# A split-precision encoder layer on one core: H in pairs of slots, three products of zeros at the start, and work moved forward on four engines

## The reference, cut to what matters

```python
h = x + W_o(sig(g_s5) * S5branch(xn) + sig(g_conv) * ConvBranch(xn))     # xn = RMSNorm(x)
h = h + CrossAttn(RMSNorm(h), RMSNorm(mem))                              # 256 rows of mem each
h = h + SwiGLU(RMSNorm(h))                                               # d_ff 2816

# S5 branch, per direction (forward, and backward with reverse=True); 32 groups of 16 channels, 64 states
A_bar = exp(A * dt);  B_bar = ((A_bar - 1) / A) * B
bu = einsum("gnp,blgp->blgn", B_bar, u)
h = scan(h[t] = A_bar * h[t-1] + bu[t])
y = einsum("gpn,blgn->blgp", C, h).real          # summed over the directions
y = gelu(y + d * u);  s5_out = (y @ w_glu_a) * sigmoid(y @ w_glu_b)
```

## Time and profile before

| | |
|---|---|
| median of 3 runs | 2540.95 us |
| the profiled execution | 2542.96 us |
| its span, mean granted TensorE clock | 2541.3 us, 0.988 |
| PE busy | 2451.0 us (96%), 12542 instructions |
| DVE, ACT, POOL busy | 1641.1, 765.8, 275.4 us (65, 30, 11%) |
| PE in the chain that ended last | 88%, DVE 3%, DMA 2% |

### The profile page before, as it was taken

How to read it: one execution, slowest core, us unless ns; L and a number is a source line. 1 busy time by engine, 2 the same in 40 slices (tenths; PEclk the granted TensorE clock), 3 DMA queues, 4 the chain that set the end, 5 groups by cost and what they waited for, 6 DMA issues and landing times.

```text
span 2541.3 us, 34409 instructions
## 1 busy us (share of the span) xinstructions
PE 2451.0 (96%) x12542; PEld 2201.0 (87%) x12542; DVE 1641.1 (65%) x2978; ACT 765.8 (30%) x1226; POOL 275.4 (11%) x283
## 2 busy tenths in 40 slices
PE   8999988799999999999999999999999999999997
PEld 6788866678888788888868999999999999999996
DVE  6735542358874397253264588888878687777777
ACT  5301110232222332130143244343343343332333
POOL 0078781000000021000000000010100000000000
PEclk9999998999999999999999999999999999999999
DMA  7332227542223743213231212132332621222212
GB/s 240 120 116 82 84 71 140 147 142 73 73 82 125 206 182 124 83 58 133 81 107 49 87 50 76 59 113 85 110 104 94 250 68 58 88 82 79 77 69 73
DMA packets 103801, 262.99 MB, mean 103 GB/s; under 512 B 15104, under 2 KB 46336, under 8 KB 103680
## 3 DMA queue, kind: packets, MB, share of 16 engines
q1 hardware_dynamic: 96736, 238.82, 29.1%
q0 software_dynamic: 6944, 22.55, 2.6%
HBM read 198.45 MB, written 64.98 MB: 104 GB/s over the span
## 4 chain that ended last, share of the span: by engine, by line
PE 88%; DVE 3%; DMA 2%; issue 1%; ACT 1%; SPq 0%; DVEq 0%; ACTq 0%
PE bank L735 27%; PE bank L737 27%; PE bank L736 27%; PE bank L1013 2%; PE bank L959 2%; PE bank L990 1%; DMA BBL<-scratch_BB 1%; PE bank L956 1%; PE bank L1002 0%; DVE EL L2133 0%; ACT EH L1176 0%; DVE HR L2446 0%; PE bank L901 0%; DMA ML<-scratch_M 0%; SPq L413 0%
## 5 line engine op out<-in xcount | busy, mean ns | idle before, releaser
L735 PE MATMUL bank<-XN,WLO 128*128 128x512 f32 x1152 | 449.3, 390 | 3.7 <-DVE WLO L1639 1.7
L737 PE MATMUL bank<-XN,WHI 128*128 128x512 f32 x1152 | 448.2, 389 | 0.0
L736 PE MATMUL bank<-XN,WHI 128*128 128x512 f32 x1152 | 448.2, 389 | 0.0
L735 PE MATMUL bank<-XH,EL 128*128 128x384 f32 x1232 | 412.4, 335 | 1.6 <-DVE U2T L2159 0.9
L737 PE MATMUL bank<-XH,EH 128*128 128x384 f32 x1232 | 411.5, 334 | 0.0
L736 PE MATMUL bank<-XL,EH 128*128 128x384 f32 x1232 | 411.5, 334 | 0.0
L735 PEld LDWEIGHTS bank<-XN,WLO 128*128 128x128 f32 x1152 | 216.2, 188 | 50.2 <-issue 3.1
L736 PEld LDWEIGHTS bank<-XN,WHI 128*128 128x128 f32 x1152 | 216.2, 188 | 45.1 <-issue 0.5
L737 PEld LDWEIGHTS bank<-XN,WHI 128*128 128x128 f32 x1152 | 216.2, 188 | 45.0
L735 PE MATMUL bank<-AF,EL 128*128 128x384 f32 x704 | 238.3, 338 | 9.7 <-DVE AF L1644 6.4
L736 PE MATMUL bank<-AF,EH 128*128 128x384 f32 x704 | 236.5, 336 | 0.0
(11 more groups left out here) (267 smaller groups left out, 3888.4 us busy)
## 6 DMA issues: line engine op xcount, KB each, us to landing
RAW<-W_all SPq DMA_DIRECT2D x132, 512.0 KB, 3.5
WR<-W_all SPq DMA_DIRECT2D x92, 512.0 KB, 4.5
scratch_G<-GS SPq DMA_DIRECT2D x16, 768.0 KB, 3.7
XS<-xT SPq DMA_DIRECT2D x8, 768.0 KB, 6.0
scratch_CO<-COS SPq DMA_DIRECT2D x8, 768.0 KB, 4.3
COL<-scratch_CO SPq DMA_DIRECT2D x8, 768.0 KB, 4.3
G2L<-scratch_G SPq DMA_DIRECT2D x8, 768.0 KB, 5.8
G1L<-scratch_G SPq DMA_DIRECT2D x8, 768.0 KB, 7.2
```

The source lines that it names most:

```text
L735: pe_mm(out, w[1], x[0], start=first, stop=False, skip_group_check=onto)
L736: pe_mm(out, w[0], x[1], start=False, stop=False, skip_group_check=onto)
L737: return pe_mm(out, w[0], x[0], start=False, stop=last, skip_group_check=onto)
```

## The change

- PE issues three products of zeros (128x512, f32) ahead of the first key product; DVE zeroes their operand first.
- DVE: the seven parts of the parameters stand between steps of kv (n is the slot), not behind it. ACT's two Sin stand in kv too.
- POOL: the first direction's loads of B and C are issued before the powers, the second's after its buffers are free.
- H holds pairs of slots, `[pair, column, 2]`: two neighbouring slots lie side by side. The copies into H are four per side instead of two (odd and even slots apart), the scan's operands have a stride of 8 bytes, the products of s5b read both slots of a pair, and ML's two products of 128 and 64 columns are one of 192. s5b's results go to banks 4 to 7, not 0 to 3.
- SP: the loads of s5a's first two iterations are issued in co, those of the others two iterations ahead. y comes back from DRAM in halves of a tile, YL lies elsewhere, and the parts of y's first tile lie in XN, so that it is split before s5b is through. The last iteration of glu is unrolled on ACT and DVE.
- FFN: in the last step of each group (`close=True`), the gated product of block 0 is made and split inside the step.

```diff
-    H = at("H", 0, [SLOTS, GD])
+    H = at("H", 0, [PAIRS, GD, 2])
...
+    def states_of(g, slot, n, odd):
+
+        pairs = slice((slot + 1 + odd) // 2, (slot + 1 + odd) // 2 + n // 2)
+        return H[:, pairs, bass.ds(g, 2), 1 - odd].rearrange("p s g -> p g s")
...
+    def y_part(low, k):
+
+        return YHL[:, low, k] if k else XN[:, low, KT - 1]
...
+        def load_v(it, par):
+            g = bass.ds(2 * it, 2)
+            sp.dma_start(VN[:, par], V_d[:, g, :, :].rearrange("p g d c -> p (g d) c")).then_inc(S(f"s5a_in{par}"), 16)
+
+        def load_w(it, par):
+            g = bass.ds(2 * it, 2)
+            sp.dma_start(WK[:, par].rearrange("p (g d) c -> p g d c", d=2),
+                         W_d[:, g, :].rearrange("p g (d c) -> p g d c", d=2)[:, :, :, 0:P]
+                         ).then_inc(S(f"s5a_in{par}"), 16)
+            sp.dma_start(BBL[:, par].rearrange("p (d g) c -> p d g c", d=2),
+                         BB_d[:, :, g, :].rearrange("d p g c -> p d g c")).then_inc(S(f"s5a_in{par}"), 16)
...
+            if j == 2:
+                for par in range(2):
+                    sp.wait_ge(S(f"tables_stored{par}"), 2 * 4 * 32)
+                sp.wait_ge(S("bb_stored"), 32)
+                for par in range(2):
+                    load_v(par, par)
+                    load_w(par, par)
...
-                if not (last and par):
-                    sp.wait_ge(S("states_bwd"), it)
-                    s5a_loads(it + 1, 1 - par)
+                if not last:
+                    sp.wait_ge(S("v_turned"), it + 1)
+                    load_v(it + 2, par)
+                    sp.wait_ge(S("lags"), it + 1)
+                    load_w(it + 2, par)
...
-        def load_y(k):
-
-            sp.wait_ge(S(f"y_stored{k}"), 32)
-            for g in range(P // GP):
+        def load_y(q):
+
+            k, half = q // 2, q % 2
+            sp.wait_ge(S(f"y_stored{k}"), 16 * (half + 1))
+            for g in range(4 * half, 4 * half + 4):
                 sp.dma_start(YL[GP * g:GP * (g + 1), k], y_rows[8 * k + g]).then_inc(S(f"y_in{k}"), 16)
...
         for q in range(quads):
+            if q:
+                load_y(q - 1)
             sp.wait_ge(S("y_made"), 2 * (q + 1))
             g = slice(QUAD * q, QUAD * (q + 1))
             sp.dma_start(Y_d[:, g, :], U[:, g, :]).then_inc(S(f"y_stored{q // 2}"), 16)
             if q + 2 < quads:
                 s5b_loads(q + 2)
-            if q % 2 == 0 and q:
-                load_y(q // 2 - 1)
...
+        for dst, src in ((BX, "BX"), (BY, "BY"), (CX, "CX"), (CY, "CY")):
+            pool.dma_start(dst[:], io[src][0]).then_inc(S("bc_in"), 16)
...
                 pool.wait_ge(S("bb_stored"), 16)
-            for dst, src in ((BX, "BX"), (BY, "BY"), (CX, "CX"), (CY, "CY")):
-                pool.dma_start(dst[:], io[src][d]).then_inc(S("bc_in"), 16)
-            pool.wait_ge(S("bc_in"), 64 * (d + 1))
+                pool.wait_ge(S("bc_in"), 96)
+                for dst, src in ((CX, "CX"), (CY, "CY")):
+                    pool.dma_start(dst[:], io[src][1]).then_inc(S("bc_in"), 16)
+            else:
+                pool.wait_ge(S("bc_in"), 64)
...
+            if d == 0:
+                for dst, src in ((BX, "BX"), (BY, "BY")):
+                    pool.dma_start(dst[:], io[src][1]).then_inc(S("bc_in"), 16)
...
+                    if d:
+                        pool.wait_ge(S("bc_in"), 128)
...
+        pe.wait_ge(S("vector_step"), 1)
+        for _ in range(3):
+            nc.tensor.matmul(PS[5][:], SQ[:, 0, 0:P], SQ[:, 0, 0:BLK], start=True, stop=True)
         key(0)
         key(1)
...
-                        pe.wait_ge(S("y_made"), 2 * (q - 1) + n + 1)
-                    out = PS[2 * par + n][:, g % 2 * NC:(g % 2 + 1) * NC]
-                    u = one(U, QUAD * q + g)
-                    for c0, n, slot in ((0, NCP, 0), (NCP, NCS, SLOT_S)):
-                        o = out[:, c0:c0 + n]
-                        nc.tensor.matmul(o, ML[par][:, g, :], u[:, c0:c0 + n], start=True, stop=False)
-                        for d in (1, 0):
-                            h = H[:, slot:slot + n, bass.ds(d * GROUPS + QUAD * q + g, 1)].rearrange("p s o -> p (s o)")
-                            last = nc.tensor.matmul(o[:, ::-1] if d else o,
-                                                    WO[par][:, g, d, :], h, start=False, stop=d == 0)
+                        pe.wait_ge(S("y_made"), 2 * q + n - 3)
+                    out = PS[4 + 2 * par + n][:, g % 2 * NC:(g % 2 + 1) * NC]
+                    nc.tensor.matmul(out, ML[par][:, g, :], one(U, QUAD * q + g), start=True, stop=False)
+                    for d in (1, 0):
+                        for c0, n, slot in ((0, NCP, 0), (NCP, NCS, SLOT_S)):
+                            o = out[:, c0:c0 + n]
+                            h = H[:, slot // 2:(slot + n) // 2, bass.ds(d * GROUPS + QUAD * q + g, 1), :]
+                            last = nc.tensor.matmul((o[:, ::-1] if d else o).rearrange("p (s t) -> p s t", t=2),
+                                                    WO[par][:, g, d, :], h.rearrange("p s o t -> p s (o t)"),
+                                                    start=False, stop=d == 0 and c0 > 0)
...
+        yin = lambda k, b: (y_part(0, k)[:, blk(b)], y_part(1, k)[:, blk(b)])
+        pe.wait_ge(S("y_made"), GROUPS // 2 - 2)
         first_half_pair("glu", lambda k: (S("y_lo"), k + 1), yin)
...
+            if n == KT + 4:
+                act.wait_ge(S("angles"), 2)
+                nc.scalar.activation(PA[:, 9, :], PA[:, 9, :], ACT.Sin).then_inc(S("sines"), 1)
+                nc.scalar.activation(PA[:, 10, :], PA[:, 10, :], ACT.Sin).then_inc(S("sines"), 1)
...
-            dst = H[:, :, bass.ds(d * GROUPS + 2 * it, 2)].rearrange("p s g -> p g s")
             src = src[:, 0:2 * NC].rearrange("p (g c) -> p g c", g=2)
-            for lo, n, c in ((1, NCP, 0), (SLOT_S + 1, NCS, NCP)):
-                copy(dst[:, :, lo:lo + n], src[:, :, c:c + n]).then_inc(signal, 1)
+            for slot, n, c in ((0, NCP, 0), (SLOT_S, NCS, NCP)):
+                for odd in range(2):
+                    dst = states_of(d * GROUPS + 2 * it, slot, n, odd)
+                    copy(dst, src[:, :, c + odd:c + n:2]).then_inc(signal, 1)
...
+        def y_split(k):
+
+            act.wait_ge(S(f"y_in{k}"), 128)
+            copy(y_part(0, k).rearrange("p (c t) -> p c t", t=C), YL[:, k].rearrange("p t c -> p c t")
+                 ).then_inc(S("y_hi"), 1)
+
         for it in range(GROUPS // 2):
             act.wait_ge(S("s5_out"), it + 1)
-            nc.scalar.activation(U[:, 2 * it:2 * it + 2, :], PS[it % 4][:, 0:2 * NC].rearrange(
+            nc.scalar.activation(U[:, 2 * it:2 * it + 2, :], PS[4 + it % 4][:, 0:2 * NC].rearrange(
...
+            if it == GROUPS // 4:
+                y_split(0)
...
+                if isinstance(i, int) and par:
+                    act.wait_ge(res, RES0["glu"] + 6 * KT)
...
+        with loop(nc.scalar, 3) as i:
+            glu(i)
+        glu(3)
...
+                if close and j == 6:
+                    act_hi(s, odd, 0)
...
+        then(V.memset(SQ[:, 0, 0:BLK], 0.0))
...
+            if n == 6:
+                parameters(0)
+                parameters(1)
+            if n == KT + 3:
+                parameters(2)
             if n == KT + 4:
                 values_out(0)
+            if n == KT + 5:
+                parameters(3)
+                parameters(4)
+            if n == 2 * KT - 1:
+                parameters(5)
+                parameters(6)
...
-        for part in range(5):
-            parameters(part)
...
-            if j == 0:
-                parameters(5)
-                parameters(6)
...
-            then(V.memset(H[:, slot, :], 0.0))
+            then(V.memset(H[:, slot // 2, :, 0], 0.0))
...
+            def seqs(s, p0=0, p1=P):
+                a = H[p0:p1, bass.ds(pair + s // 2, SLOT_S // 2 + 1 if both else 1), :, s % 2]
+                return a[:, ::SLOT_S // 2, :] if both else a
-            nxt = seqs(H, slot + 1)
-            scan.up(V.tensor_tensor(S1[:, 0:n, :], seqs(H, slot), wide(LR), ALU.mult))
...
-            scan.up(V.tensor_tensor(S2[0:half, 0:n, :], seqs(H, slot, half, P), wide(LI, half, P), ALU.mult))
-            scan.up(V.tensor_tensor(S2[half:P, 0:n, :], seqs(H, slot, 0, half), wide(LI, 0, half), ALU.mult))
...
             dve.wait_ge(scan.sem, real)
             scan.up(V.tensor_tensor(nxt, nxt, S1[:, 0:n, :], ALU.add))
             dve.wait_ge(scan.sem, scan.n)
             scan.up(V.tensor_tensor(nxt, nxt, S2[:, 0:n, :], ALU.add))
...
                     with_first(UP1, 3, U3T, (S("summed"), 5 * s + 2), j, s)
+                    if close:
+                        gated(s, 0)
                 if j == 6:
+                    if close:
+                        gated_lo(s, odd, 0)
...
+                             q + 8 if g == 0 else None, q + 9, 0, close=True)
...
```

(18 more changed lines are left out.)

103 lines of the change are left out of this document (40 added, 63 removed).

## The result

The changed kernel takes 2499.48 us, the median of 4 runs (2496.65 to 2499.55); the kernel before takes 2541.32 in the runs beside it (2539.57 to 2543.29). The ratio is 0.9832, 95% interval 0.9815 to 0.9849: 41.8 us faster, where 61 were forecast. The forecast of 2480 and its range up to 2496 both missed, on the slow side. The span of the profiled execution fell from 2541.3 to 2497.8, by 43.5.

A forecast was written before the change was run, and what follows sets the result against it. TensorE, busy 96% of the span, was taken as the bound, leaving its waits, low clock and instruction lengths. 0 + 0.4 + 23.3 + 17.5 + 7 + 5 + 7.5 = 60.7 off 2542.96 gave 2482.3, median 2480; range 2470 to 2496.

The forecast's parts named there:

- E: s5b: paired reads of H and one ML of 192 columns take a quad from 7.4 to 6.4 us; 7 us gained.
- G: FFN close: earlier gated product of block 0 cuts waits for AF and low clock in both groups; 7.5 us gained.
- A: Start of kv: three products of zeros gain 0, since TensorE waits for the sum of squares anyway; bounds 1.0 either way.
- Rival 5: Start of kv: zeros bring full clock and the sum of squares moves forward too; 2.4 us, 2478; chance 0.07.
- B: Parameters moved into kv slots: a stall of about 1.3 against a WLO wait of 1.7 gone; net gain 0.4 us.
- C: POOL starts earlier and its load waits go, so TensorE's 22.2 us stall at CIN is covered; 23.3 us gained.
- Rival 1: POOL's tables come late and 11 us of the stall at CIN remain: 2491; chance 0.15.
- D: s5a: earlier loads remove the waits for BBL, less some clock and copy losses; 17.5 us gained, bounds 9 and 20.
- Rival 3: s5a: PSUM copies of every second element take half a us longer per iteration; 8 us, 2488; chance 0.12.
- rival 2: s5b is held by its loads, quads stay at 7.4 us and y comes no earlier: 2490; chance 0.15.
- F: y and glu: y's low part made during s5b, loads in halves; the 6.2 us wait goes; 5 us gained, bounds 2 and 9.
- H: Scan: VectorE reads and writes H at a stride of 8 bytes in place of 4; no change, 290 ns.

The follow-up runs named there:

- e6: The changed kernel without the three products of zeros: 2498.97 us, ratio 0.9826.
- e11: The changed kernel with all seven parts of the parameters and the two Sin back behind kv: 2511.78 us, ratio 0.9874.
- e4: The changed kernel with own WO and ML buffers for each quad of s5b, loads issued further ahead, TensorE's quad loop unrolled: 2486.62 us, ratio 0.9779.
- e1: The changed kernel with the close only in FFN group 1, group 0 as in the kernel before: 2496.14 us, ratio 0.9827.
- e2: The changed kernel with the loads of XH and XL number 6 issued behind the RAW load that group 1's first step needs: 2493.29 us, ratio 0.9811.
- e3: The changed kernel with only a quarter of each low part XL loaded for group 1: 2492.27 us, ratio 0.9802.
- e9: The changed kernel with ScalarE waiting for the last store of QS behind its first exponentials, not ahead: 2497.96 us, ratio 0.9826.

## Why the prediction was wrong, step by step

The direction was right and the size some 40% too large (60.7 us forecast, 43.5 measured in the span). Two terms of the sum failed, E and G, and one that was put at nothing, attention ("All else stays, the FFN and attention stages above all"). Step by step:

- A (zeros, 0): right, by e6. Rival 5 held as to the products' speed (0.47 for 0.77 at 8.26) and failed as to the time: TensorE then waits for the operands (3.8 us in three waits for MN) and for the sum of squares (1.2), both VectorE's.
- B (0.4): the stall of 1.3 came, to the tenth (1.28 for VVS); the wait of 1.7 for WLO fell to 0.3. Kv ended 1.9 later, not 1.3, which is within what it differs by from trace to trace.
- C (23.3): right, 21.6 with A and B, where 23.7 stood; e11 shows the mechanism. POOL started 1.1 late and the table was there at 367.8, not 367.0, later than the 367.5 at which it was due. It was still half a us early (2.91 less 2.40), since the 0.8 that TensorE takes there by itself wasn't in that sum; this 0.8 lies inside the 1.0 left as a rest. Rival 1 didn't come.
- D (17.5): right, 18.7. Waits for BBL are 2.4 in all, where under 2 were to be left. Rival 3 (reads of every second element) cost nothing that the iteration shows (3.0 to 3.1 us for 3.12). "The stage over by 512" was no test of this sum: 532.71 less 0.4, 23.3 and 17.5 is 491.5, and it was over at 492.42.
- E (7): the step that failed is "5.0 us to landing plus some 1.7 from the quad's end to the issue plus the next but one's 5.2, over two quads, is 5.95", of which the sum took 6.4. The chain was the right one, and two of its three links too short: 6.5 us to landing, not 5.0, and 6.6 for the quad behind the wait, not 5.2, since the granted clock was 0.59 in its first 4.1 us (763.38 to 767.50); from the end to the issue it was 1.6. With 0.2 from the landing to the product that is 14.8 per two quads in place of 12.8. Those are the old 7.4 a quad: the outcome of rival 2, which had 0.15, and the stage gained 0.8 of the 7. The products themselves came out better than priced (1.22 a group for 1.30). e4 shows that it was the chain: with more buffers the same bytes go at 233 GB/s and the stage takes 45.9 us. I had priced what the faster engine saves, and taken the landing time from a trace in which TensorE waited for ML only once, 1.5 us. The wait for quad 1, 3.7 for 1.5 before, wasn't in the sum at all.
- F (5): right, 5.4 (the wait of 6.2 less the 0.8 that glu to q grew). The wait of 6.2 went, one of 2.1 came, as forecast; E and F together gave 6.2 in place of 12.
- G (7.5): group 1 gave its 2.0 (given as 1.9 a sentence before the sum). In group 0 "Of 4.5 some 1.4 remain" was right (1.2), and the step from there to the time failed: that a wait and the low clock behind it, once gone, are gained. What is late next was not asked for: the row of 1992.1 in the earlier trace rows shows DMA at 1.02 and 422 GB/s, and I read only its clock. I counted 5.5 where the transfers had 1.2 us to give (RAW landed at 2013.7 and was read at 2014.90). A wait of 4.45 came back behind them, with 7 us at a granted clock of 0.57, and the stretch took 69.2 for 67.9. e1 to e3 show it.
- Attention (put at nothing): 3.7 lost where nothing was changed. e9 shows through which wait. ScalarE waited for this store in the trace of before as well (1267.43), where it landed in 3.3 us; that it would land after 5.7 can't be seen there.
- H (0): right, 291 ns. Rival 4 didn't come.

By size: E and F 5.8, G 6.7, attention 3.7, A to C 2.1, less 1.2 of D, make 17.1 of the 17.2 by which the span missed (60.7 forecast, 43.5 measured). The range was too narrow for this: E and G had bounds of their own in the text (0 and 3; G's 0.8 was below its bound) and attention had none, but I let the rivals come "one at a time", and three things failed together.

The Trainium skill, TensorE: Matmul & The Clock Gate, section "Part 1: The HAM clock gate", says that the default state is throttled and activity releases it. The durations agree (0.77 without zeros in e6, 0.47 with them), and no time followed from it. The Trainium skill, SBUF — State Buffer, section "The DMA port swizzle", has lines of 16 bytes that need two hits for full bandwidth. VectorE's 291 ns at a stride of 8 agree. TensorE's eight records of H in a group, at single elements 256 bytes apart, took 1.34 us (0.86, and 0.48 from 799.79 to 800.27); in pairs they take 0.84.
